# Two transformer blocks on one core: the setup rearranged, with weights loaded behind x, positions and one gain row turned on their own, and the two angle tables moved

## What is computed

```python
for l in range(2):
    h = rmsnorm(x, g_pre_mix[l])
    zf, zq, zk, zv, zm = split(h @ w_in[l])           # 1024 -> 1280
    y_f = fourier_mix(zf, w_fourier[l])
    q, k = rope(zq, positions), rope(zk, positions)   # angle = position * frequency; cos and sin
    y_a = window_attention(q, k, zv, sink[l])
    km, vm = split(rmsnorm(mem, g_mem[l]) @ w_mem_kv[l])
    y_m = memory_attention(zm, km, vm)
    ...                                               # output projection, feed-forward
...                                                   # the second block, two layers
```

## Time and profile before

| | us |
|---|---|
| median of 3 runs (3453.3 to 3456.86) | 3453.76 |
| the profiled execution, its own time | 3453.98 |
| its span, first to last instruction | 3452.2 |
| PE busy | 3361.5 (97% of the span) |
| DVE busy | 2450.0 (71%) |
| ACT busy | 1623.8 (47%) |

### The profile page before, as it was taken

How to read it: one execution, slowest core, us unless ns; L and a number is a source line. 1 busy time by engine, 2 the same in 40 slices (tenths; PEclk the granted TensorE clock), 3 DMA queues, 4 the chain that set the end, 5 groups by cost and what they waited for, 6 DMA issues and landing times. The chain is left out here.

```text
span 3452.2 us, 49516 instructions
## 1 busy us (share of the span) xinstructions
PE 3361.5 (97%) x19557; PEld 2884.6 (84%) x19557; DVE 2450.0 (71%) x3500; ACT 1623.8 (47%) x2399; POOL 67.0 (2%) x96
## 2 busy tenths in 40 slices
PE   7999999999999999999999999999999989999999
PEld 5679988768998899887678899889988757788997
DVE  8669854759882888567895698559864888658863
ACT  4545643455562556226523365436542562335642
POOL 1000000000000000000000000000000000000000
PEclk9999999999999999999999999999999999999999
DMA  4123323213333333332132333333333213323332
GB/s 142 50 73 111 103 94 110 82 49 95 106 114 97 91 111 111 100 101 58 50 98 87 109 98 111 101 107 99 111 104 97 76 44 94 90 98 98 111 104 86
DMA packets 341371, 325.25 MB, mean 94 GB/s; under 512 B 31960, under 2 KB 312356, under 8 KB 341156
## 3 DMA queue, kind: packets, MB, share of 16 engines
q1 hardware_dynamic: 335588, 307.95, 28.1%
q0 software_dynamic: 3776, 12.45, 1.6%
q10 hardware_dynamic: 1792, 1.88, 0.2%
HBM read 313.84 MB, written 2.10 MB: 92 GB/s over the span
## 5 line engine op out<-in xcount | busy, mean ns | idle before, releaser
L2171 DVE TENSOR_TENSOR w_lo<-raw,w_hi 128x2048 fp32r<-128x2048 f32 x190 | 435.2, 2290 | 481.9 <-ACT w_hi L1525 481.4
L1525 ACT ACTIVATE w_hi<-raw 128x2048 fp32r<-128x2048 f32 x190 | 363.8, 1915 | 832.8 <-PE products L800 579.6
L800 PE MATMUL products<-a_hi,w_hi 128*128 128x512 f32 (+1 forms) x1216 | 489.9, 403 | 12.6 <-DVE a_lo L2231 9.9
L800 PE MATMUL products<-a_hi,w_lo 128*128 128x512 f32 (+1 forms) x1216 | 476.1, 392 | 0.0
L800 PE MATMUL products<-a_lo,w_hi 128*128 128x512 f32 (+1 forms) x1216 | 475.6, 391 | 0.0
L941 PE MATMUL products<-seven_x,w_hi 128*128 128x256 f32 x2592 | 466.4, 280 | 8.4 <-ACT h_full L1637 5.8
L941 PEld LDWEIGHTS products<-seven_x,w_hi 128*128 128x128 f32 x2592 | 396.2, 188 | 11.3 <-ACT h_full L1637 7.0
L941 PE MATMUL products<-seven_x,more_hi 128*128 128x256 f32 x1632 | 375.9, 279 | 0.3
L941 PE MATMUL products<-seven_x,w_lo 128*128 128x256 f32 x1296 | 362.7, 280 | 0.0
L800 PEld LDWEIGHTS products<-a_hi,w_hi 128*128 128x128 f32 (+1 forms) x1216 | 229.2, 188 | 69.5 <-issue 16.5
L941 PEld LDWEIGHTS products<-seven_x,more_hi 128*128 128x128 f32 x1632 | 278.0, 188 | 1.5 <-ACT rs_b L1637 1.5
(11 more groups left out here) (465 smaller groups left out, 7229.7 us busy)
## 6 DMA issues: line engine op xcount, KB each, us to landing
raw<-in_ffn_w SPq DMA_DIRECT2D x244, 512.0 KB, 4.1
raw<-in_w_in SPq DMA_DIRECT2D x108, 512.0 KB, 4.6
raw<-in_w_ffn_in SPq DMA_DIRECT2D x88, 512.0 KB, 4.2
raw<-in_w_ffn_out SPq DMA_DIRECT2D x40, 512.0 KB, 4.5
raw<-in_w_out SPq DMA_DIRECT2D x32, 512.0 KB, 4.0
raw<-in_ffn_w SPq DMA_DIRECT2D x24, 384.0 KB, 3.4
x_sums<-x_sums POOLq DMA_DIRECT2D x12, 512.0 KB, 6.0
raw<-in_w_mem_kv SPq DMA_DIRECT2D x8, 512.0 KB, 4.0
```

Source lines behind the costliest of these rows:

```text
L800: mm = pe.matmul(G[pair][0:m, into + b, 0:n], w[:, s, at:at + m], x, start=(first or into > 0) and k == 0 and q == 0, stop=(last or ends) ...
L1525: act.activation(w_hi[:, s, :], raw[:, s, :], ACT.Copy).then_inc(hi_ready, 1)
L2171: dve.tensor_tensor(w_lo[:, s, :], raw[:, s, :], w_hi[:, s, :].bitcast(F32), ALU.subtract).then_inc(lo_ready, 1)
```

## The change

SP issues the first two weight units right behind x, and 20 of the small parameter loads after them; 12 small loads and the three constants go to POOL's queue, 3 stay with ACT. The memsets of `raw` go; a small memset releases `lo_ready`. The one gain row that the first unit needs is loaded and turned by itself into `first_gain`; the five tiles of `rows` are turned after the first unit. Positions are loaded as 128 by 4 numbers instead of broadcast, cast and repeated by DVE, and turned by PE into bank `B7`. DVE makes the first table before it copies any of x, copies six chunks of x instead of eight (ACT copies two), and mixes copies with low halves. x is turned into eight banks, from the fourth chunk on after the table has read `B7`. The first unit multiplies its high halves of the first three chunks before it needs `w_lo`. Twenty products of a matrix of ones are put between the other work of PE. The second table moves on DVE from behind the squares of x to behind the scaling of `zkv`; the scaling of the queries and the fourth `w_lo` move ahead of the memory chunks; ACT's cosine moves behind them.

```diff
+        x_banks = [B4[:], B5[:], B6[:], B7[:], G[1][:, 0, :], G[1][:, 1, :], B4[:], B5[:]]
+        on_scalar = 6
+        sp_rows, pool_rows, act_rows = row_loads[:20], row_loads[20:32], row_loads[32:]
...
-            sp.wait_ge(rows_zeroed, 1)
-            for dst, src in row_loads[1::2]:
-                sp.dma_start(dst, src).then_inc(rows_loaded, 16)
...
                 tall("w_in", l, 2 * P)
+                if l == 0:
+                    sp.wait_ge(rows_zeroed, 1)
+                    for dst, src in sp_rows:
+                        sp.dma_start(dst, src).then_inc(rows_loaded, 16)
...
+            def first_unit():
+
+                take_hi_only()
+                terms = [(b, k, q) for k in range(3) for b in range(2) for q in range(2)]
+                terms += [(b, k, 2) for k in range(3) for b in range(2)]
+                terms += [(b, k, q) for k in range(3, DC) for b in range(2) for q in range(3)]
...
+            def ones_products(n):
+
+                for _ in range(n):
+                    pe.matmul(G[0][:, 1, 0:P], ones[:], ones[:], start=True, stop=True)
+
+            pe.wait_ge(sq_used, 1)
+            ones_products(6)
+            pe.wait_ge(pos_cast, 1)
             pe.wait_ge(ident_loaded, 16)
+            for tc in range(TC):
+                mm = pe.transpose(B7[:, tc * P:(tc + 1) * P], angles[:, 2, tc * P:(tc + 1) * P], ident[:])
+            mm.then_inc(pos_spread, 1)
+            pe.wait_ge(gain_row_loaded, 16)
+            pe.transpose(G[0][:, 0, 0:P], X[:, 0, 0:P], ident[:]).then_inc(gain_turned, 1)
+            ones_products(6)
...
+                if i == 3:
+                    pe.wait_ge(angle, 1)
                 for tc in range(TC):
-                    mm = pe.transpose((B4, B5)[i % 2][:, tc * P:(tc + 1) * P], x_tok[:, tc, i * P:(i + 1) * P], ident[:])
+                    mm = pe.transpose(x_banks[i][:, tc * P:(tc + 1) * P], x_tok[:, tc, i * P:(i + 1) * P], ident[:])
                 mm.then_inc(turned, 1)
...
-            act.dma_start(angles[:, 0, :].bitcast(I32), t["positions"][0].partition_broadcast(P)).then_inc(
+            act.wait_ge(gain_row_zeroed, 1)
+            act.dma_start(X[0:DC, 0, 0:P], t["g_pre_mix"][0].rearrange("(c p) -> c p", p=P)).then_inc(gain_row_loaded, 16)
+            act.dma_start(angles[:, 0, 0:TC].bitcast(I32), t["positions"][0].rearrange("(t p) -> p t", p=P),
+                          allow_slow_non_contiguous=True).then_inc(
                 pos_loaded, c.one("pos_loaded", 16))
             constant(freq, "freq", pos_loaded)
...
+                    for i in range(4):
+                        first_high(i)
                     split_hi()
+                    for i in range(4, DC):
+                        first_high(i)
...
-                    sine(sinT, angles)
-                    sine(cosT, angles)
+                    params_copied()
...
-            for s in range(2):
-                dve.memset(raw[:, s, :], 0.0).then_inc(lo_ready, 1)
-            for i in range(DC):
+            dve.memset(tiny[:, 2, :], 0.0).then_inc(lo_ready, 2)
...
+            dve.wait_ge(pos_loaded, c.next("pos_loaded", 32))
+            dve.tensor_copy(angles[:, 2, :].rearrange("p (t e) -> p t e", t=TC),
+                            angles[:, 0, 0:TC].bitcast(I32).unsqueeze(2).broadcast_to([P, TC, P])).then_inc(pos_cast, 1)
+            dve.wait_ge(pos_spread, 1)
+            stepped(dve.tensor_scalar(angles[:, 1, :], B7[:], freq[:, 0:1], None, ALU.mult))
+            settled()
             rope_table(0.0, angles)
...
                 if l == 0:
-                    dve.wait_ge(sin_done, c.next("sin_done"))
-                    rope_table(0.25, angles)
-                    dve.wait_ge(sin_done, c.next("sin_done"))
+                    dve.wait_ge(turn_copied, 2)
                 piece()
                 split_lo()
                 inverse_rms(rs, D)
                 scaled(zkv[:], group(), rs)
+                if l == 0:
+                    dve.wait_ge(sin_done, c.next("sin_done"))
+                    rope_table(0.25, angles)
+                    piece()
+                    scaled(qT[:, 0:2, :], group(), rs)
+                    split_lo()
                 begin_sum()
                 for i in range(DC):
                     dve.wait_ge(ah_ready, c.next("ah_ready"))
...
-                piece()
-                scaled(qT[:, 0:2, :], group(), rs)
-                split_lo()
+                if l == 0:
+                    dve.wait_ge(sin_done, c.next("sin_done"))
```

More of the change, by code:

```diff
@@ L313, in two_blocks @@
     x_tok = place("x_tok", [P, TC, D], at=REGION_B)
+    rows = place("rows", [P, n_param_tiles, P], at=REGION_B + 20 * KB)
     y_tok = place("y_tok", [P, TC, D], at=REGION_B)
@@ L548, in two_blocks @@
         n_setup_loads = 3
+        first_gain = tiny[:, 5, :]
+        x_banks = [B4[:], B5[:], B6[:], B7[:], G[1][:, 0, :], G[1][:, 1, :], B4[:], B5[:]]
+        on_scalar = 6
+        sp_rows, pool_rows, act_rows = row_loads[:20], row_loads[20:32], row_loads[32:]
         block = stack.enter_context(nc.Block())
@@ L1093, in all_read_out, with take_hi_only @@
                     pe.wait_ge(read_out[p], c.now(f"read_out{p}") + 1)
-            pe.wait_ge(ident_loaded, 16)
+            def first_unit():
[3 more added lines that the diff above has]
+                terms += [(b, k, q) for k in range(3, DC) for b in range(2) for q in range(3)]
+                pair = c.group % 2
+                pe.wait_ge(read_out[pair], c.next(f"read_out{pair}"))
+                for b, k, q in terms:
+                    if (b, q) == (0, 0):
+                        pe.wait_ge(al_ready, c.next("al_ready"))
+                    if (b, k, q) == (0, 0, 2):
+                        pe.wait_ge(lo_ready, c.next("lo_ready"))
+                    w, x = ((w_hi, a_hi), (w_hi, a_lo), (w_lo, a_hi))[q]
+                    at = k * 2 * P + b * P
+                    mm = pe.matmul(G[pair][:, b, :], w[:, 0, at:at + P], x[:, k, :],
+                                   start=k == 0 and q == 0, stop=k == DC - 1 and q == 2)
+                mm.then_inc(piece_done, 1)
+                c.group += 1
+            def take_hi_only():
+                pe.wait_ge(hi_ready, 1)
+                c.unit += 1
+            def ones_products(n):
[4 more added lines that the diff above has]
+            pe.wait_ge(pos_cast, 1)
+            pe.wait_ge(ident_loaded, 16)
+            for tc in range(TC):
[4 more added lines that the diff above has]
+            ones_products(6)
             for i in range(DC):
@@ L1099, in _, with turn_rows @@
                     pe.wait_ge((x_loaded, x_rest_loaded)[i // (DC // 2)], 16)
-                if i >= 2:
-                    pe.wait_ge(xt_copied, i - 1)
+                if i >= 6:
+                    pe.wait_ge(xt_copied, i - 5)
+                if i == 3:
+                    pe.wait_ge(angle, 1)
                 for tc in range(TC):
-                    mm = pe.transpose((B4, B5)[i % 2][:, tc * P:(tc + 1) * P], x_tok[:, tc, i * P:(i + 1) * P], ident[:])
+                    mm = pe.transpose(x_banks[i][:, tc * P:(tc + 1) * P], x_tok[:, tc, i * P:(i + 1) * P], ident[:])
                 mm.then_inc(turned, 1)
[L1105 to L1108, removed]
-                else:
[L1110 to L1115, removed]
+            ones_products(8)
+            def turn_rows():
+                pe.wait_ge(rows_loaded, 16 * (len(sp_rows) + len(act_rows)))
+                pe.wait_ge(more_rows_loaded, 16 * len(pool_rows))
+                pe.wait_ge(xt_scalar, DC - on_scalar)
+                for i in range(n_param_tiles):
+                    bank = (B4, B5)[i // 4]
+                    pe.transpose(bank[:, i % 4 * P:(i % 4 + 1) * P], rows[:, i, :], ident[:]).then_inc(turned, 1)
+            for l in range(DEPTH):
+                if l == 0:
+                    first_unit()
+                    turn_rows()
+                else:
+                    full(fresh="al_ready")
                 if l == 0:
@@ L1842, in _ @@
             act.wait_ge(rows_zeroed, 1)
-            for dst, src in row_loads[0::2]:
+            for dst, src in act_rows:
                 act.dma_start(dst, src).then_inc(rows_loaded, 16)
-            constant(rot_pe, "rot_pe", consts_loaded)
-            constant(causal, "causal", consts_loaded)
-            act.dma_start(sinks[:], t["sink"].rearrange("l h -> (l h)").partition_broadcast(P)).then_inc(consts_loaded, 16)
             def sine(table, tile=X):
@@ L1874, in _ @@
                 c.apart(act)
+                if l == 0:
+                    unit_done()
                 for i in range(DC):
@@ L1877, in _ @@
                     square(memT[:, i, :], MEM)
-                unit_done()
+                if l == 0:
+                    sine(cosT, angles)
+                else:
+                    unit_done()
                 group_skipped()
@@ L2770, in _ @@
             dve.wait_ge(pool_step, 2)
+            dve.memset(X[:, 0, 0:P], 0.0).then_inc(gain_row_zeroed, 1)
```

(7 more changed lines are left out.)

61 lines of the change are left out of this document (48 added, 13 removed).

## The result

The changed kernel takes 3463.64 us (median of 22 runs, 3457.91 to 3469.39); the kernel before took 3456.69 beside it (22 runs, 3451.65 to 3461.74). The ratio is 1.0019, interval 1.0013 to 1.0025: slower by 6.9 us, just at the bound of 0.2%. The forecast was 3455.8 within 3451 to 3461, so the time lies outside the range. It is 7.8 us over the forecast. Of these, 2.9 are the kernel before, whose median lies that much above that of its first three runs; the other 4.9 are the difference between the two kernels, 6.9 where 2.0 was forecast, and they are what the experiments look for.

The account below looks back on a forecast made before the run. PE is busy nearly throughout, so time can be won only where it waits or runs at its lower clock, within the first 80 us. 3.9 won up to `zkv`, 5.8 lost behind: 1.9 slower than 3453.98, 3455.8, range 3451 to 3461.

Parts of the forecast that it names:

- The landmark: Start of the key rotation on DVE, 64.50 before; forecast at 66.4, 1.9 us later.
- When DVE can start: DVE's opening wait for positions and frequencies: landing taken as 9.5 us, bounds 5.2 and 13.
- The first table: DVE's first angle table: 5.7 us plus about 0.8 for PE's turn, done at 16.0 instead of 20.9.
- To the first product: Copies, low halves and high halves after the first table: PE starts at 22.9 instead of 24.22.
- The first unit: PE's first weight unit: ends at 34.9, midway between 33.8 at full clock and 35.9 at the low one.
- the ones do nothing: Rival on PE's clock: it falls all the same, sum 1.0 worse, 3456.8; inside "no change", no chance of its own.
- The second unit: PE from 35.5 to the spreading at 46.2 (before 50.04); `zkv` ends at 49.3, 3.9 us ahead.
- Behind `zkv`: DVE from `zkv` to key rotation: 17.1 us against 11.35, with PE waiting some 6 us.
- won up to `zkv`: Forecast gain of 3.9 us by the end of `zkv`, before 5.8 are lost behind it.
- The rival that ended slower: Positions land very late, holding all of DVE: passes 0.2% from a landing at 14.6; 3462 at 15.7; chance 0.11.
- signs of being wrong: DVE's cast starting before 7 or after 13 us, or PE not waiting at the third unit's memory sums.
- an estimate of 11.5 for the landing: Positions' load as 512 pieces by the page's rule: 5.4 us transfer, landing near 11.5, sum 3457.9.

Follow-up runs that it names:

- Both experiments with the second table: Changed kernel with the second table back behind the squares of x: 1.0004; kernel before with only that table's move and its accompanying reordering: 1.0016; both against the kernel before.
- the last version: Changed kernel with the three repairs and the identity on SP's queue ahead of x (also "the identity apart"): 3453.24 us, 0.9987 of the kernel before.
- the single runs: Changed kernel with one repair each, ratios to the kernel before: second table back 1.0004, sine's table loaded early 1.0008, positions and frequencies issued first 1.0010.
- the three repairs: Changed kernel with second table back behind the squares, sine's table loaded early, and positions and frequencies issued first, together: 0.9998 of the kernel before.

## Why the prediction was wrong

The landmark was forecast at 66.4 and came at 70.51. The 4.1 us are found step by step:

- **When DVE can start** is the largest miss: a landing of 9.5 was assumed, and the cast began at 11.46, +2.0. The forecast argued that 256 KB less ahead of the frequencies would bring them in earlier; but they were issued 0.6 us later, behind the gain row, and took 9.2 us instead of 8.5. The positions took 3.1, 6.0 or 8.2 us by what was issued ahead of and beside them, while broadcasting them instead changed the landing by about 1 us.
- **The first table** took 7.1 instead of 6.5 (+0.6): the turn left DVE idle for 1.21 us, and the multiply reads PSUM at 0.75.
- **To the first product**: 8.0 us from the table's end instead of 6.9 (+1.1). The term left out was ACT's table load; with it taken away the product came 1.1 earlier. The sequence "sine, then the high halves" was in the code; that a load of 1.28 us goes with the sine, and starts only when the sine's own wait is over, was not priced. Before, the sine and its load stood behind the first product, at 35.85 to 37.8. The Trainium skill, "ScalarE: Activation LUTs", section "What ACT_TABLE_LOAD costs", gives 1283 ns for the load and 1380 ns more for a drain. The trace agrees on the load; of a drain on the path nothing shows, since the sine follows 1.29 us after the load's start.
- **The first unit** took 12.7 instead of 12.0 (+0.7): the middle between the two clocks was too kind, as the low stretch came with the ones too. That the ones do nothing was a rival with a price of 1.0; the run without them is 0.6 longer here, less than executions with the ones differ by, so what they are worth stays open.
- **The second unit**, from the row tiles' end (39.95) to the spreading, took 11.0 instead of 10.7 (+0.3), and from there to the end of `zkv` 3.0 instead of 3.1.
- **Behind `zkv`** the mechanism and nearly the size were right: 16.5 us instead of 17.1 to the key rotation, a wait of PE of 6.3 where some 6 was forecast, at the memory sums and released by DVE. Both experiments with the second table confirm it for the table; 1.2 of the loss stay without it, with the queries and the `w_lo`, whose place the forecast gave no price.

2.0, 0.6, 1.1, 0.7, 0.3, -0.1 and -0.6 make 4.0. The failed step is thus the estimate of the first product, 22.9 against 26.57, made of three terms that all erred to the same side; with it the 3.9 us "won up to `zkv`" became 0.8 lost. A further 0.6 came between the key rotation and the fifth unit, a stretch with the lower clock in both kernels (a mean of 0.50 at 70 to 74 us, after PE's long wait, and before the change 0.57 at 66 to 70).

The rival that ended slower named the right place, the late start, but needed a landing beyond 14.6. The time came out on its side at 11.46, because the other terms were added to it. Its size rested on one view, the time from issue to landing before; the terms that were not in that view had no range. Neither of the signs of being wrong came (the cast lies between 7 and 13, and PE waits at the memory sums): they watched the mechanism behind `zkv` and the landing, not the way from the landing to the first product.

The rule of the Trainium skill on non-contiguous loads ("DMA: Bandwidth & Descriptors", "Rules for kernel authors") led the prediction to an estimate of 11.5 for the landing, and 11.46 was measured. The agreement is in the number alone, and luck: the broadcast form landed only 1 us sooner, and with the identity ahead of x the pieces landed in 3.1 us, less than the 5.4 that this estimate has for their transfer alone. The same page's section "Issuing engines are not separate DMA queues" says that transfers of all engines run on the same 16 DMA engines and interleave; the traces agree, as the positions, first on ACT's queue both times, landed after 6.0 us with x issued on SP's queue at the same moment and after 3.1 with the identity ahead of x.

## What to carry to other kernels

When a list is made to begin with a wait for a small load, ask first what is issued ahead of it and beside it on every queue: its landing is set by its neighbours, and giving each of the first-needed loads the head of a queue was worth more here than what was tried behind them: of the 11.0 us by which the last version's key rotation is ahead of the changed kernel's, 4.1 are the table's and 1.1 the sine's by the single runs, which leaves 5.8. An instruction moved to an earlier place takes its hidden companion (here a table load) with it, and that is paid where the moved instruction waits. Work put into a chain that is already without gaps, as DVE's behind `zkv`, costs its full length there even where the total of work is unchanged (5.2 us in the kernel before, of which leaving the old place gave 1.4 back).

## What was not expected of the hardware

- 64 KB of identity issued ahead of x, which delayed x's issue by 0.45 us, cut the landing of a 2 KB load on another queue from 6.0 to 3.1 us. The run took the identity off the positions' queue and let x start later, both at once; which of the two does it was not separated.
- The first unit fell to the lower clock in all these kernels but one, with the products of ones before it or without them, and in the three repairs not at all. PE had stood 2.5 us before that unit there, as long as with the identity apart, where the granted clock was 0.50 at 21 to 23 us. No run here tells what decides it.
